# Attention masks on TensorE for the last units, 1/den products on GpSimd, and the sums of squares of four norms on TensorE

## What is computed

```python
def rms_norm(x, g):
    y = x * lax.rsqrt(jnp.mean(x * x, axis=-1, keepdims=True) + EPS)
    return y * g
...
# attention: 15 heads of 64 in three groups g of 5 slots, (window, dilation) = (128,1), (512,4), (2048,16)
q, k, v = split(h @ w_qkv); q = rope(rms_norm(q)); k = rope(rms_norm(k))
# in each residue class of the dilation a centred band |j_q - j_k| <= 64
s = where(valid, q k^T / 8, -1e30); p = exp(s - max); den = sum(p); o_g = (p / den) v; lse_g = max + log(den)
wts = softmax(stack(lse_g), axis=groups)          # per position and head slot
x = x + concat(o_g * wts_g) @ w_o
x = x + square(relu(rms_norm(x) @ w_up)) @ w_down
b, c, u = split(rms_norm(x) @ w_in); x = x + (b * conv3(c * u)) @ w_out
x = x + square(relu(rms_norm(x) @ w_up)) @ w_down
return rms_norm(x)
```

## Time and profile before

| | |
|---|---|
| median of 3 runs | 1525.1 us (1524.06 to 1525.36) |
| the run that was profiled | 1525.36 us |
| span of its slowest core (core 7) | 1523.8 us |
| spans of the 8 cores | 1516.7 to 1523.8 us |
| granted PE clock, mean over the span, by core | 0.972 to 0.977 |
| PE busy | 1454.9 us (95%) |
| DVE, ACT, POOL busy | 602.4, 490.8, 520.4 us (40%, 32%, 34%) |

### The profile page before, as it was taken

The page is one execution under the profiler, slowest core; times in us unless marked ns, Lnnn a source line. Parts: engine busy times, 40 slices in busy tenths (PEclk is TensorE's granted clock), DMA queues, the critical chain, the costliest instruction groups (busy, mean ns, idle before and its releaser), DMA issues.

```text
span 1523.8 us, 20000 instructions; the slowest of 8 cores (1516.7 to 1523.8 us)
## 1 busy us (share of the span) xinstructions
PE 1454.9 (95%) x7207; PEld 674.7 (44%) x7207; DVE 602.4 (40%) x819; ACT 490.8 (32%) x778; POOL 520.4 (34%) x492
## 2 busy tenths in 40 slices
PE   5999997699899999999999999999999999999996
PEld 2656443233344444444444444443444444444444
DVE  3646677557314013023038534457123023032057
ACT  3566686343220310310333433333310310301333
POOL 5100000135550530630665322246621621612552
PEclk8999999589999999999999999999999999999998
DMA  9944445630330420510410333311310411313014
GB/s 249 188 91 97 95 106 113 183 79 1 56 55 1 72 40 1 83 29 5 72 22 7 56 42 49 56 28 26 58 28 14 71 28 29 55 28 52 5 55 166
DMA packets 60911, 95.00 MB, mean 62 GB/s; under 512 B 3792, under 2 KB 40912, under 8 KB 58768
## 3 DMA queue, kind: packets, MB, share of 16 engines
q0 software_dynamic: 52016, 69.18, 26.6%
q1 hardware_dynamic: 8800, 24.55, 5.5%
HBM read 127.37 MB, written 8.52 MB: 89 GB/s over the span
## 4 chain that ended last, share of the span: by engine, by line
PE 89%; DVE 3%; DMA 3%; issue 2%; ACT 1%; POOL 1%; SPq 0%; DVEq 0%; ACTq 0%; POOLq 0%
PE psum L317 89%; DVE arena L336 3%; DMA arena<-scr 2%; DMA arena<-xT 2%; ACT arena L328 1%; DVE arena L333 1%; POOL arena L333 0%; POOL arena L349 0%; ACT arena L343 0%; ACT arena L433 0%; SPq L349 0%; DMA scr<-arena 0%; POOL arena L449 0%; DVE arena L345 0%; DVEq L216 0%
## 5 line engine op out<-in xcount | busy, mean ns | idle before, releaser
L317 PE MATMUL psum<-arena 128*128 128x512 bf16 (+6 forms) x7207 | 1454.9, 366 | 61.1 <-ACT arena L448 18.3
L317 PEld LDWEIGHTS psum<-arena 128*128 128x128 bf16 (+2 forms) x7207 | 674.7, 101 | 841.0 <-issue 155.5
L333 DVE TENSOR_TENSOR arena<-arena,psum 128x512 f32<-128x512 f32 (+1 forms) x384 | 258.2, 684 | 782.6 <-PE psum L317 776.1
L333 POOL TENSOR_TENSOR arena<-arena 128x512 bf16<-128x512 bf16 (+2 forms) x393 | 443.0, 1133 | 340.0 <-ACT arena L328 151.7
L328 ACT ACTIVATE arena<-psum 128x512 bf16<-128x512 f32 (+1 forms) x306 | 201.4, 669 | 639.0 <-PE psum L317 618.6
L336 DVE SCALAR_TENSOR_TENSOR arena<-arena 128x512 bf16<-128x512 f32 (+2 forms) x232 | 181.6, 840 | 29.7 <-ACT arena L328 24.9
L333 DVE TENSOR_TENSOR arena<-arena 128x2048 bf16<-128x2048 bf16 (+4 forms) x146 | 127.9, 921 | 35.3 <-ACT arena L328 25.7
L349 POOL DMA_DIRECT2D arena<-wdn x16 | 12.5, 784 | 318.9 <-PE psum L317 318.9
L433 ACT ACTIVATE arena<-arena 128x512 f32<-128x512 f32 x114 | 70.6, 631 | 153.4 <-DVE arena L333 136.2
L343 ACT CAST arena<-psum 128x512 bf16<-128x512 f32 (+2 forms) x149 | 87.2, 592 | 92.4 <-PE psum L317 87.7
L328 ACT ACTIVATE arena<-arena 128x512 f32<-128x512 f32 (+2 forms) x85 | 54.5, 659 | 65.3 <-DVE arena L333 51.0
(11 more groups left out here) (16 smaller groups left out, 38.5 us busy)
## 6 DMA issues: line engine op xcount, KB each, us to landing
arena<-wup POOLq DMA_DIRECT2D x16, 1024.0 KB, 9.9
arena<-wdn POOLq DMA_DIRECT2D x16, 1024.0 KB, 12.8
arena<-xT POOLq DMA_DIRECT2D x14, 1024.0 KB, 9.8
arena<-arena SPq DMA_DIRECT2D x14, 512.0 KB, 4.6
arena<-scr SPq DMA_DIRECT2D x14, 512.0 KB, 6.4
arena<-win POOLq DMA_DIRECT2D x8, 768.0 KB, 7.5
outT<-arena SPq DMA_DIRECT2D x24, 256.0 KB, 2.5
arena<-wqk POOLq DMA_DIRECT2D x7, 512.0 KB, 10.0
```

The costliest lines, as they stand in the source:

```text
L317: i = e.matmul(o, lhsT=l, rhs=r, start=s0, stop=s1, skip_group_check=True)
L333: return p.op(eng, lambda e: e.tensor_tensor(out=out, in0=in0, in1=in1, op=op), R, W, cost)
```

## The change

- **Norms.** `square_sum` and its buffers are gone. Every tile of every norm takes the form with bf16 squares and eight matmuls with ones.
- **Masks on PE.** For units 5, 6 and 7 (`PMU = 5`) the mask is no longer a DVE product behind the exponential. Each step begins with two 128x512 matmuls of an identity with a bias (0 where a key is seen, -30000 elsewhere) into the two score banks, and the scores are added to it. The bias comes as a new input and is loaded, at unit 5, over the mask table in SBUF (`CRM`), and the identity beside it, by two DMAs on POOL's queue. Unit 5 has 4 steps, unit 6 has 4 and 2, unit 7 has 4: 28 such matmuls.
- **Two O/den pairs.** Units 6 and 7 alternate between banks (6, 7) and (0, 1); the other units keep the one pair.
- **Unit table.** The units' groups and slots are written as a table, `UNITS`, and the list of fillers as `FILL`. The order in both is the order before. V of group 2 has priority 300 + 10 x 32 = 620 in place of 2310, and V of group 1 300 as before. `mark[7]` is three places earlier, among fillers that do nothing.
- **1/den products.** In `finalize` the products go to POOL (`FD = 0` leaves only that engine), with a cost of 0.2 + 0.0019 x 512 in the plan; for units 0 to 5 `finalize` has priority 7400 (`FP`) in place of 2000 and 5000. `dts` holds the same buffer twice.
- **The plan's costs.** The scores' cost is taken whole where masks are on PE; the extra cost of an evacuation holds only for dilation 4.
- `wo_tiles` is defined but not called (`WS = 0`).

```diff
+UNITS = [(0, 0), (1, 0), (2, 0), (0, 1), (1, 1), (2, 1)]
+FILL = "v1 p1 p2 v2 p3 p4 p5 p6 p7".split()
+
+
+FD, FP, PMU, WS = 0, 7400, 5, 0
...
+    bias_d = din("bias", [128, NCST - C_MB + 128])
...
+        ident = B(U_RS + 1024, 128)
...
-        dtot = B(U_DT, 4096, True)
+        dts = [B(U_DT, 4096, True)] * 2
...
-        def square_sum(gidx, src, c0, n, bank):
-
-            bufs = nsq[14336 if gidx == 4 else 2048]
-            acc = bufs[nq[0] % 2]
-            nq[0] += 1
+        def norm_tile(gidx, src, c0, n, bank, out_fn, pool=False):
+
             for c in range(8):
-                xa, xr = src(c)
-                t = acc
-                if c:
-                    t = bufs[2 + nq[1] % 3]
-                    nq[1] += 1
-                o, r_ = t.ap[:, 0:n], t.r(0, n)
-                p.op([("act", lambda e, o=o, i=xa: e.activation(out=o, in_=i, func=AF.Square), c_act(n, False)),
-                      ("dve", lambda e, o=o, i=xa: e.tensor_tensor(out=o, in0=i, in1=i, op=ALU.mult),
-                       c_dve(n, False))], None, [xr], [r_], None)
-                if c:
-                    d, dr = (h_ap(0, c0, n), h_r(0, c0, n)) if c == 7 else (acc.ap[:, 0:n], acc.r(0, n))
-                    TT("pool", d, acc.ap[:, 0:n], o, ALU.add, [acc.r(0, n), r_], [dr], n)
-            MMS([(PS(bank, 0, n), onesN, h_ap(0, c0, n), True, True)], [CR1, h_r(0, c0, n)], [PR(bank)])
-
-        def norm_tile(gidx, src, c0, n, bank, out_fn, pool=False, on_pe=True):
-
-            if not on_pe:
-                square_sum(gidx, src, c0, n, bank)
-            for c in range(8 if on_pe else 0):
...
-        def attention(u, g, lanes, first):
+        def attention(u, g, lanes, first, dtot, rings):
...
-            bo, bd = pO
+            bo, bd = rings[0]
...
+                    bo, bd = rings[(B_ + 1) % len(rings)]
...
-                more = 0.0 if D == 1 else 0.7
+                more = 0.7 if D == 4 else 0.0
...
+                on_pe = u >= PMU
+                if on_pe:
+                    for q in range(2):
+                        kk = kinds[0:2] if nl == 2 else kinds[2 * q:2 * q + 2]
+                        if D == 16:
+                            map_ = mask_ap(C_M16, [[0, 4], [1, 128]])
+                        elif kk == [1, 1]:
+                            map_ = mask_ap(m0 + 256, [[0, 2], [1, 256]])
+                        else:
+                            map_ = mask_ap(m0 + 256 * kk[0], [[1, 512]])
+                        mms.append((PS(sb + q), ident.ap, map_, True, False))
+                    rd += [CRM, ident.r()]
...
-                                    kv(kb.ap[hs(h)]), qv(qb.ap[hs(h)]), True, True))
+                                    kv(kb.ap[hs(h)]), qv(qb.ap[hs(h)]), not on_pe, True))
...
+                if on_pe:
+                    ml = []
+                elif D == 16:
...
-        def finalize(units, lo, n):
+        def finalize(units, lo, n, dtot):
...
-                TT("dve", o, o, dtot.ap[rows, lo:lo + n], ALU.mult, [rr, dtot.r(lo, lo + n, half)], [rr], n)
+                fn = lambda e, o=o, i=dtot.ap[rows, lo:lo + n]: e.tensor_tensor(out=o, in0=o, in1=i, op=ALU.mult)
+                p.op([("dve", fn, c_dve(n, False)), ("pool", fn, 0.2 + 0.0019 * n)][1 - FD:], None,
+                     [rr, dtot.r(lo, lo + n, half)], [rr], None)
...
-        UG = [0, 1, 2, 0, 1, 2]
-        USL = [(0, 1)] * 3 + [(2, 3)] * 3
...
+            if u == PMU:
+                DMA("pool", cst.ap[:, C_MB:NCST], bias_d[:, 0:NCST - C_MB], [], [CRM], "bias", 0,
+                    128 * (NCST - C_MB) * 4)
+                DMA("pool", ident.ap, bias_d[:, NCST - C_MB:], [], [ident.r()], "ident", 0, 1 << 16)
             q_, k_ = qk[u % 2]
             if u < 6:
-                attention(u, UG[u], [(0, USL[u][0], q_, k_), (1, USL[u][1], q_, k_)], u % 3 == 0)
-                if u % 3 == 2:
+                g, pr = UNITS[u]
+                mine = [i for i in range(6) if UNITS[i][1] == pr]
+                attention(u, g, [(0, 2 * pr, q_, k_), (1, 2 * pr + 1, q_, k_)], u == mine[0], dts[pr], [pO])
+                if u == mine[-1]:
+                    p.pri = FP
                     for tt in range(4):
-                        finalize([u - 2, u - 1, u], tt * 512, 512)
+                        finalize(mine, tt * 512, 512, dts[pr])
             elif u == 6:
-                attention(6, 1, [(0, 4, q_, k_)], True)
-                attention(6, 2, [(1, 4, q_, k_)], False)
+                attention(6, 1, [(0, 4, q_, k_)], True, dts[0], [pO, (0, 1)])
+                attention(6, 2, [(1, 4, q_, k_)], False, dts[0], [pO, (0, 1)])
             else:
-                attention(7, 0, [(0, 4, q_, k_)], False)
+                attention(7, 0, [(0, 4, q_, k_)], False, dts[0], [pO, (0, 1)])
...
-        fill = v_tiles(1, 300)
-        mark = {0: 3}
-        fill += proj_tiles(1)
-        mark[1] = len(fill) + 3
-        fill += proj_tiles(2)
-        mark[2] = len(fill) + 3
-        fill += v_tiles(2, 2310)
-        for u in range(3, 8):
-            fill += proj_tiles(u)
-            mark[u] = len(fill) + 3
+        def wo_tiles(tt):
+            def one(oc):
+                p.pri = 7500
+                b = pp.next()
+                wo_mm(b, oc, tt, range(6), 2)
+                add_x(tt, oc, 0, 512, b)
+            return [lambda oc=oc: one(oc) for oc in range(8)]
+
+
+
+        fill, mark = [], {0: 3}
+        for what in FILL:
+            if what[0] == "v":
+                fill += v_tiles(int(what[1]), 300 + 10 * len(fill))
+            else:
+                fill += proj_tiles(int(what[1]))
+                mark[int(what[1])] = len(fill) + (3 if what != "p7" else 0)
...
-            norm_tile(gidx, lambda c: xs(tt, c, lo, n), tt * 512 + lo, n, 7, fn, on_pe=n < 512)
+            norm_tile(gidx, lambda c: xs(tt, c, lo, n), tt * 512 + lo, n, 7, fn)
...
+    bias = np.concatenate([-30000.0 * (1.0 - cst[:, C_MB:NCST]), np.eye(128)], axis=1).astype(np.float32)
```

## The result

The changed kernel takes 1551.1 us (1549.7 to 1555.4); the kernel before, run beside it, 1524.9. The ratio is 1.0177, with an interval of 1.0157 to 1.0198: 26 us slower, where 1521.5 (1508 to 1536) was forecast. The profiled run is one of 1549.69 us, with a span of 1548.1 on core 5.

A forecast was written before the change was run, and what follows sets the result against it. TensorE was taken to bound the kernel, 95% busy, with the weak place at the end of attention, at half clock. Attention terms of -14.6 and norms of +11 gave -3.6 on 1525.1: 1521.5 us, range 1508 to 1536.

The forecast's parts named there:

- the start of unit 6: End of attention: rotary chain 6 and unit 6 start 10 us earlier (2 to 14), plus 1.8 from V's priority.
- the price of the products on GpSimd: Attention, 1/den products moved off DVE: twelve take 16 us on GpSimd (14 to 17); projections cover unit 3's wait.
- The wait for the bias itself: Unit 5: scores wait for the bias DMA until about 241.5, covered by projection work, counted as nothing (5 us uncovered).
- The waits for the bank pair: Units 6 and 7: a second O/den pair removes 6 of the 7.7 us idle in 274:308.
- The clock: Units 6 and 7: TensorE's clock comes back for half of the tail, -9 us.
- the half-clock rival: Units 6 and 7: clock stays 0.50 to the end, 20 mask matmuls cost 8.6 us; 1530.5 us, chance 33%.
- the full-clock rival: Units 6 and 7: masks and missing waits keep or bring the clock up throughout; 1512 us, chance 20%.
- The norms: Norms 1 to 4: 105 added matmuls cost 22.8 us, 11.4 given back; +11 us (3.5 to 23).
- V's priority: Attention before 250 us: earlier V of group 2 may remove 1.8 us idle; -1.8, other end 0.
- The den buffer: Unit 6's first den evacuation waits for GpSimd's last product: +1 us; as a rival 1529.5 us, chance 7%.

## Why the prediction was wrong, step by step

Two steps failed most: the start of unit 6, which is most of the miss, and the price of the products on GpSimd, which is the first in time.

**The products on GpSimd.** The prediction priced them by GpSimd's own time (14 to 17 us) and asked only who waits for them; projections were to cover that. It did not ask what runs on DVE meanwhile, although it used the very same slowdown for the norms, from the earlier trace rows, where scalings beside GpSimd's adds take 8.81 us in place of 5.9. Twelve GpSimd products made unit 3's rotary chain late and PE stop for 5.4 us; in the kernel before all 32 cost 17 us, and twelve idle ones 12. That DVE was given back 7.3 us was true and worth nothing there: unit 3's chain began at 180.3, when its row swap had landed, and at 180.5 in the trace of the kernel before, behind the products.

**The start of unit 6** was to be 11.8 us earlier (1.8 and 10) and is 14.0 later. This one term is 25.8 of the 29.6 by which the forecast missed. Its parts are 8.5 for the chain's write of 1/rms, 1.2 for the read-back and 4.3 on DVE. Of the 8.5, the longer stop ahead of unit 3 is 3.6 (5.4 where 1.8 were idle), and the mask edit alone makes the same write 4.6 later (254.45 where it was 249.87). The step said that chain 6 would start earlier by unit 5's wait for the bias. It came later with unit 5: unit 5's first scores were at 247.1 (forecast 241.5, and 237.7 before), and half of the sums of chain 6 (four matmuls at 255.7) stand on PE behind the last of them. No row had shown that the chain could go on during that wait. The read-back then took 17.6 us beside the load; that this collision stays, the step had said. In the kernel with the masks alone it is worse by another way: there the write fell behind the load and took 12 us, with no product on GpSimd, and unit 6 began at 280.0. So this step fails without the products as well.

**The wait for the bias itself** was right: PE has no gap worth naming from 195.3 to 259, and unit 7's projection covers it. What it costs is behind it, in chain 6.

**The waits for the bank pair** went, as forecast (6 of 7.7): 0.6 us idle in 285:331. **The clock** did not come back for half of the tail, it came for none: 0.50 to 331. That is the 9 us of the sum, with the sign of the half-clock rival, whose 8.6 for 20 mask matmuls is what they cost. Its 1530.5 was too low mostly by the start of unit 6. The step took the mask matmuls, being of the form that ran when the clock rose, for a possible help; they were none. Against the full-clock rival it put the empty stretch; the run that filled it shows that this was not the only reason.

**The norms** were forecast at 11 (3.5 to 23) and measured 7.2 (8.2 by the ratios) and 7.8: the mechanism and the sign were right, the part given back was mis-sized, about 15 of the 22.8 us added where 11.4 was the forecast. At the boundaries the longest stall is now 1.0 us twice and none at the second, and the low clock there is gone:

```profile
PE psum L326 <- ACT arena L337: 2.7, 3, 1.0
```

**V's priority** was to give 1.8 and cost some 1.5 (0 to 3). **The den buffer** did not hold unit 6: GpSimd's last product ended before unit 6's first scores, which DVE held.

In sum: 25.8 from the start, 9 from the clock and -4 from the norms make 30.8, where the forecast missed by 29.6; the smaller terms make the difference.

## What to carry to other kernels

Before an operation goes to an idle GpSimd, list what DVE does in the same microseconds: two-input products on both took about as long side by side as one after the other, and once a single DVE product was held for 6.5 to 13 us by a run of GpSimd's. The price is paid by DVE's chain. When a wait is to move a chain forward, name the instructions of the chain that lie in it; here they came later with the unit that waited. Work out a step that is moved for every small DMA of the chain behind it: a transfer of 16 KB issued just behind a 1 MB load took 12 us here. And after a wait is taken away, name the next one on the same path from its own chain (here unit 7's key copy), not from what is left of the old one.

## What was not expected of the hardware

PE was busy for 45.4 of 46 us at 0.50 in the changed kernel (285 to 331), and with matmuls of 128 by 128 placed right ahead of unit 6 the clock still fell from 1.00 to 0.56 in 12.9 us of unbroken work. Twelve GpSimd products that no engine waits for cost the kernel 11.8 us, and one DVE product, 1.22 us alone, took 9.37 us while GpSimd's products beside it ran on at 1.15 each.
